# Seven-product block multiplication for the MLP of a one-step decoder layer, with split activations kept in DRAM

## What is computed

```python
x = x + gt1 * mix                                   # mix = merged @ w_out
h = _rmsnorm(x, g2n) * (1 + sc2) + sh2
x = x + gt2 * (jnp.square(jax.nn.relu(h @ w_up)) @ w_down)
...
y_prompt = _rmsnorm(xp, g_final)                    # y_sample the same
```

## Time and profile before

| | us |
|---|---|
| median of 3 runs (1808.34 to 1810.19) | 1808.41 |
| span of the profiled execution | 1804.3 |
| PE busy | 1775.4 (98%) |
| DVE busy | 759.9 (42%) |
| ACT busy | 489.3 (27%) |
| POOL busy | 12.3 (1%) |
| DMA, mean over the span | 77 GB/s |

### The profile page before, as it was taken

The page is one execution under the profiler, slowest core; times in us unless marked ns, Lnnn a source line. Parts: engine busy times, 40 slices in busy tenths (PEclk is TensorE's granted clock), DMA queues, the critical chain, the costliest instruction groups (busy, mean ns, idle before and its releaser), DMA issues.

```text
span 1804.3 us, 26783 instructions
## 1 busy us (share of the span) xinstructions
PE 1775.4 (98%) x10976; PEld 1713.8 (95%) x10976; DVE 759.9 (42%) x1445; ACT 489.3 (27%) x832; POOL 12.3 (1%) x25
## 2 busy tenths in 40 slices
PE   8999999999999999999999989999999999999997
PEld 3899999999999999999999989999999999999997
DVE  3644324444544545333353564343333333433345
ACT  5443333223333233211232341212121121212122
POOL 0000000000000000000000010000000000000000
PEclk9999999999999999999999989999999999999999
DMA  9444544322331232211132111111111111111112
GB/s 310 141 138 156 176 130 131 83 60 69 88 97 54 63 98 58 58 47 46 49 88 79 47 36 47 48 48 46 46 37 45 46 46 46 46 46 46 47 47 97
DMA packets 192677, 139.34 MB, mean 77 GB/s; under 512 B 15323, under 2 KB 176007, under 8 KB 192630
## 3 DMA queue, kind: packets, MB, share of 16 engines
q1 hardware_dynamic: 185910, 130.01, 24.4%
q10 hardware_dynamic: 6720, 8.67, 1.4%
...
## 4 chain that ended last, share of the span: by engine, by line
PE 95%; DVE 2%; DMA 1%; issue 1%; ACT 1%; SPq 0%; DVEq 0%; ACTq 0%
PE PB L916 85%; PE M L844 3%; PE M L969 1%; PE M L860 1%; PE M L1044 1%; DMA araw<-in_w_ada 1%; PE M L1050 1%; PE M L1036 1%; PE M L1038 1%; DVE XL L1223 1%; PE M L908 0%; PE M L1014 0%; DVE R L1709 0%; ACT A L532 0%; PE M L1061 0%
## 5 line engine op out<-in xcount | busy, mean ns | idle before, releaser
L916 PE MATMUL PB<-XH,whi 128*128 128x352 f32 x2496 | 811.3, 325 | 4.1 <-DVE XL L1223 2.1
L916 PE MATMUL PB<-XH,wlo 128*128 128x352 f32 x2496 | 801.5, 321 | 0.0
L916 PE MATMUL PB<-XL,whi 128*128 128x352 f32 x2496 | 801.3, 321 | 0.0
L916 PEld LDWEIGHTS PB<-XH,whi 128*128 128x128 f32 x2496 | 469.0, 188 | 11.3 <-issue 6.9
L916 PEld LDWEIGHTS PB<-XL,whi 128*128 128x128 f32 x2496 | 470.2, 188 | 0.7
L916 PEld LDWEIGHTS PB<-XH,wlo 128*128 128x128 f32 x2496 | 468.7, 188 | 0.0
L550 ACT ACTIVATE whi<-raw 128x1024 fp32r<-128x1024 f32 x134 | 141.3, 1054 | 407.4 <-PE PB L916 404.3
L916 PE MATMUL PB<-AH,whi 128*128 128x352 f32 x720 | 233.1, 324 | 0.2 <-issue 0.2
L916 PE MATMUL PB<-AL,whi 128*128 128x352 f32 x720 | 232.5, 323 | 0.0
L916 PE MATMUL PB<-AH,wlo 128*128 128x352 f32 x720 | 232.1, 322 | 0.0
L1228 DVE TENSOR_TENSOR wlo<-raw,whi 128x1024 fp32r<-128x1024 f32 x134 | 163.7, 1222 | 118.0 <-ACT whi L550 117.1
...
## 6 DMA issues: line engine op xcount, KB each, us to landing
...
```

What stands on the lines that cost most here:

```text
L916: ins = pe.matmul(PB[:, bank, 0:BLK], w[:, w0:w0 + P], x[:, k, a0:a1], start=(k == 0 and j == 0), stop=(k == n_k - 1 and j == 2))
```

## The change

Phase 5 is written anew. The 1056 columns are two halves of 528 (`HALF`), and pairs of feature tiles stand on both sides of a product, so that weights and activations are 2 x 2 blocks. Seven block products replace the eight. With weights A11, A12 (the second half of the inputs), A21, A22 (the second output tile), and inputs B11, B12 (second half of the columns), B21, B22 (second half of the features):

- weight sums (POOL, `sums`, `last_sum`, in place in WR and WS_): S1 = A21 + A22, S3 = A11 - A21, S2 = S1 - A11, S4 = A12 - S2
- input sums: T1 = B12 - B11, T3 = B22 - B12, T2 = B22 - T1, T4 = B21 - T2
- products, numbered 0 to 6: A11 B11, S2 T2, S3 T3, S1 T1, A12 B21, A22 T4, S4 B22. Each is split in high and low and is 2 column parts of 264 (`SUB`) x k-tiles x 3 matmuls (`part`, L1497). There are four accumulators of two banks (`acc`), taken in the order `ACC`: product 4 adds onto 0, 5 onto 2, 6 onto 3.
- results: c11 = acc 0 behind product 4. `s1_copy` (ACT) copies product 0 to UB, `u2` (DVE) adds product 1, `v1` makes U3 = product 2 + UB, `t22` adds product 3 (second tile, second half); `t21` = acc 2 + UB behind product 5, `t12` = acc 3 + UB behind product 6.

**Up** has 16 pairs p (256 inner features each), 4 k-tiles a product: 7 x 24 matmuls. The results B11, B12, B21, B22 get Relu and Square on ACT (`relu2`). POOL makes from them the four differences TB1 to TB4 (`x_sums`, L735), the input sums of the down products. ACT (`bhi`, `thi`) and DVE (`blo`, L2145) split all seven (index XPOS in XS), and SP stores each, 540 KB, to DRAM (`store_x`, L540). **Down** has 8 groups g of 4 pairs d of output tiles (block P0 = 16 + 4g + d), 2 k-tiles a product: 7 x 12 matmuls. Its 14 inputs a group (540 KB each) are loaded back (`load_xd`, L568) into one of two buffers. Results are added in SBUF (AO, UACC). The first column half's residual is read back from DRAM (xm_d, stored in phase 4) by `load_a` (L602) in group 0, the second half's (X2) near the end. Weight parts are 512 (up) or 256 (down) columns, seven a pair.

**Norm.** The sum of squares is now a product of ones with SQA and SQ as the moving side, so that it stands in all partitions, 352 columns; ACT takes the root and DVE the reciprocal over 352 columns (RSTD). DVE and POOL scale A by it and form the seven inputs of the first pairs (`hb`, `xlo`, and the order `XSEQ`); the first pair takes its products in the order `FIRST`. **Output.** All nine row groups stand behind the last product, with four buffers.

The sizes, the transfers, the engines' bodies and TensorE's part (SP, POOL, ACT, DVE, PE in this order):

```diff
+HALF = T // 2
+SUB = HALF // 2
+UP, DOWN = 16, 32
+ACC = (0, 1, 2, 3, 0, 2, 3)
+XPOS = (1, 5, 4, 3, 2, 6, 0)
+FIRST = (0, 4, 2, 1, 3, 5, 6)
+XSEQ = [(0, k) for k in range(4)] + [(4, k) for k in range(4)] + [(i, k) for k in range(4) for i in (2, 1)] + \
...
+        def store_x(p, i, done):
+            sp.wait_ge(s["xl5"], 7 * p + done)
+            sp.dma_start(xd_d[bass.ds(p, 1), :, i + 1, :].rearrange("o p n -> (o p) n"),
+                         XS[:, XPOS[i]].rearrange("p x n -> p (x n)")).then_inc(xbo if done <= 3 else xto, 16)
...
+        def load_xd(g, b, i, free):
+            sp.wait_ge(s["pd5"], free)
+            sp.wait_ge(xbo, 48 * (2 * g + 2 if isinstance(g, int) else UP))
+            sp.wait_ge(xto, 64 * (2 * g + 2 if isinstance(g, int) else UP))
+            for k in range(2):
+                sp.dma_start(xd(b, i)[:, k].rearrange("p x n -> p (x n)").bitcast(F32),
+                             xd_d[bass.ds(2 * g + k, 1), :, i + 1, :].rearrange("o p n -> (o p) n")).then_inc(xdi[b], 16)
...
+        with sp.Fori(1, UP - 1) as p:
+            up(p)
+        p = UP - 1
+        sp.wait_ge(s["wl5"], 7 * UP)
+        load_down(0, 0, 0, 0)
+        load_down(1, 1, 0, 1)
+        store_t(p - 1)
+        for i in range(7):
+            load_xd(0, 0, i, 7 * p + i // 2 + 1)
+            if i == 4:
+                store_x(p, 6, 1)
+        store_x(p, 0, 2)
+        store_x(p, 4, 3)
+        store_t(p)
...
+                sp.dma_start(AO[:, n, 0:HALF], xm_d[n, :, 0:HALF]).then_inc(res_in[d % 2], 16)
...
+                if isinstance(g, int) and g == 0:
+                    load_a(d)
+                    if d == 0:
+                        for i in range(7):
+                            load_xd(1, 1, i, 7 * UP - 7 + (7 + i) // 2 + 1)
+                elif d == 0 and not last:
+                    for i in range(7):
+                        load_xd(g + 1, 1 - b, i, 7 * (P0 - 1) + i + 1)
...
+            pool.tensor_tensor(s1, a(1, 0), a(1, 1), ALU.add).then_inc(s["sum5"], 1)
+            link("sum5", pool.tensor_tensor(a(1, 0), a(0, 0), a(1, 0), ALU.subtract), 4 * P0 + 2)
+            link("sum5", pool.tensor_tensor(s2, s1, a(0, 0), ALU.subtract), 4 * P0 + 3)
...
+            for j, (out, a, b) in enumerate(((TB1, B12, B11), (TB2, B22, B12), (TB3, B22, TB1), (TB4, B21, TB3))):
+                if not first:
+                    pool.wait_ge(s["xl5"], 7 * (p - 1) + 4 + j)
+                if j >= 2:
+                    pool.wait_ge(s["tt5"], 4 * p + 2 * j - 3)
+                pool.tensor_tensor(out, a, b, ALU.subtract).then_inc(s["tt5"], 1)
...
+                x_sums(p - 1)
+            up_sums(p + 1)
+            up_last_sum(p + 1)
...
+            act.activation(RSTD[:, a0:a1], rms_psum(b), ACT.Sqrt, bias=epsc[:, 0:1], scale=1.0 / D).then_inc(s["rms_sqrt"], 1)
...
+        def relu2(p, n, buf):
+            act.activation(buf, buf, ACT.Relu).then_inc(s["rl5"], 1)
+            act.wait_ge(s["rl5"], 3 * p + n)
+            act.activation(buf, buf, ACT.Square).then_inc(s["b5"], 1)
...
+            if not first:
+                up_hi(p, 6)
+                act.wait_ge(s["c12c"], p)
+                relu2(p - 1, 3, B12)
+                s1_copy(p, UB[:])
+                thi(p - 1)
+            w(0)
+            act.wait_ge(s["t22c"], p + 1)
+            if first:
+                act.wait_ge(s["xl2"], len(XSEQ))
+            relu2(p, 1, B22)
+            bhi(p, 6, B22, 1)
+            for i in range(1, 4):
+                w(i)
+            act.wait_ge(s["pd5"], prod(p, 4))
+            if not first:
+                act.wait_ge(s["tt5"], 4 * (p - 1) + 1)
+            act.activation(two(B11), acc(0), ACT.Relu).then_inc(s["c11c"], 1)
+            act.wait_ge(s["c11c"], p + 1)
+            act.activation(B11, B11, ACT.Square).then_inc(s["b5"], 1)
+            bhi(p, 0, B11, 2)
+            w(4)
+            act.wait_ge(s["c21c"], p + 1)
+            relu2(p, 2, B21)
+            bhi(p, 4, B21, 3)
+            w(5)
...
+            dve.reciprocal(RSTD[:, a0:a1], RSTD[:, a0:a1]).then_inc(s["rstd_done"], 1)
...
+            dve.tensor_tensor(two(UB[:]), acc(1), two(UB[:]), ALU.add).then_inc(s["u2c"], 1)
...
+            dve.tensor_tensor(two(B22), acc(2), two(UB[:]), ALU.add).then_inc(s["v1c"], 1)
...
+            dve.tensor_tensor(two(B22), acc(3), two(B22), ALU.add).then_inc(s["t22c"], 1)
...
+            dve.tensor_tensor(two(B21), acc(2), two(UB[:]), ALU.add).then_inc(s["c21c"], 1)
...
+            dve.tensor_tensor(two(B12), acc(3), two(UB[:]), ALU.add).then_inc(s["c12c"], 1)
...
+        def blo(p, i, src):
+            dve.wait_ge(s["xh5"], 7 * p + XPOS[i] + 1)
+            dve.tensor_tensor(XS[:, XPOS[i], 1, :].bitcast(F32R), src, XS[:, XPOS[i], 0, :], ALU.subtract).then_inc(s["xl5"], 1)
...
+            if not first:
+                t12(p - 1)
+                up_lo(p, 6)
+                blo(p - 1, 3, TB1)
+                blo(p - 1, 2, TB2)
+                u2(p)
+                blo(p - 1, 1, TB3)
+                blo(p - 1, 5, TB4)
+                v1(p)
+            w(0)
+            if not first:
+                t22(p)
+            blo(p, 6, B22)
+            for i in range(1, 4):
+                w(i)
+            blo(p, 0, B11)
+            t21(p)
+            w(4)
+            blo(p, 4, B21)
+            w(5)
...
+        def add_gated(n, a):
+            return stt(two(out_half(n, 0)), acc(a), gate(n), two(out_half(n, 0)), ALU.mult, ALU.add)
...
+        FREE = [("c11c", 0), ("u2c", 0), ("c21c", 0), ("c12c", 0), ("s1c", 1), ("v1c", 1), ("t22c", 1)]
...
+        def turn_of(P0, i):
+            pe.wait_ge(s["wl5"], 7 * P0 + i + 1)
+            name, n = FREE[i]
+            if not (isinstance(P0, int) and P0 + n == 0):
...
+        def part(i, u, k, w, x, n_k):
+            for j, (wx, xx) in enumerate(((0, 0), (0, 1), (1, 0))):
+                ins = pe.matmul(acc(ACC[i])[:, u, :], w[wx], x[xx], start=(i < 4 and k == 0 and j == 0),
+                                stop=(k == n_k - 1 and j == 2), skip_group_check=i >= 4)
+            return ins
...
+        def down(g, b):
+            for d in range(4):
+                P0 = UP + 4 * g + d
+                for i in range(7):
+                    if d == 0 and i == 0:
+                        pe.wait_ge(xdi[b], 112 * (g - b) + 224)
+                    turn_of(P0, i)
+                    for u in range(2):
+                        for k in range(2):
+                            ins = part(i, u, k, [d_split(i, x, d % 2)[:, k, :] for x in range(2)],
+                                       [xd(b, i)[:, k, x, SUB * u:SUB * u + SUB] for x in range(2)], 2)
+                    ins.then_inc(s["pd5"], 1)
```

More of the change, by code:

```diff
@@ L504, in layer_kernel @@
+        down(0)
+        down(1)
+        with pool.Fori(1, 3) as t:
+            down(2 * t)
+            down(2 * t + 1)
+        down(6)
+        down(7, last=True)
     POOL_STEPS = 11
@@ L1668, in phase4 @@
                     lo(T4_ + n + 2, x)
[L1669 to L1670 removed]
+                if not (isinstance(i, int) and n == 0):
+                    scaled(n - 1)
                 dve.wait_ge(s["sq_done"], n + 1)
@@ new lines, in _ @@
+        for i in range(6):
+            up_lo(0, i)
+        dve.wait_ge(s["xtr_copy"], KT)
+        residual(KT - 1, 0)
+        scaled(KT - 2)
+        rstd(0)
+        residual(KT - 1, 1)
+        up_lo(0, 6)
+        rstd(1)
+        hb(0, 0)
+        hb(1, 0)
+        residual(KT - 1, 2)
+        xlo(0, 0)
+        hb(2, 0)
+        xlo(0, 1)
+        hb(3, 0)
+        xlo(0, 2)
+        rstd(2)
+        xlo(0, 3)
+        dve.wait_ge(s["rstd_done"], 3)
+        hb(7, 0)
+        hb(0, 1)
```

997 lines of the change are left out of this document (612 added, 385 removed).

## The result

The changed kernel takes 1863.71 us (median of 4 runs, 1858.29 to 1869.97) where the kernel before takes 1808.74; the ratio is 1.0305, 95% interval 1.0282 to 1.0327. The direction was forecast, the size was not: +55 us instead of +8, outside the range that ended at 1836. The profiled execution has a span of 1868.2 us, so it is one of the longer runs.

What follows compares the result with a forecast made beforehand. TensorE's work was taken to bound the kernel before, a three-engine ring the new up loop; -89.5 + 41 + 19 + 18 + 14 + 2.5 + 3 = +8 gave 1816 us, range 1800 to 1828, 8 in 10 1768 to 1836.

Steps and rivals of the forecast that it cites:

- So TensorE sets the pace: Down: a product block takes TensorE 10.1 us, other engines less, and loads at 240 GB/s stay under 360.
- TensorE's work: Whole MLP: 5376 matmuls of 264 columns at 0.1206 us replace 4608 of 352 columns, -89.5 us.
- the hole that was forecast: Down group 0: residual rows stand behind 14 loads for group 1, so TensorE waits, +14 us (+6 to +18).
- the up loop: Up pairs 1 to 15: a three-engine ring takes 22.7 us a pair against TensorE's 20.3, +41 us (+15 to +55).
- the clock: Behind two long gaps the granted clock falls to the 1.2 GHz level for a while, +3 us (0 to +6).
- VectorE's ring: Up loop: path from t12 to next t12 through VectorE, ScalarE and GpSimd, 20.7 us, or 22.7 with locks.
- The stretching by GpSimd: Up loop: VectorE operations with two SBUF inputs wait for whole GpSimd operations, +2.0 us a pair.
- start and bridge: MLP start: norm and first splits, +19 us; between up and down: TensorE waits for 14 loads, +18 us.
- the tail: Behind the last product: all output row groups stand there, 20 us instead of 17.5, +2.5 us (0 to +5).
- Rival 1: Up loop: TensorE still sets the pace, a pair takes 20.7 us, 1769 us in all; chance 0.35.
- Rival 2: Up stores and down loads: DMA becomes the bound below 240 GB/s, bridges grow by 20, 1848 us; chance 0.07.
- Rival 3: TensorE: 264-column matmuls start only every 0.13 us, 27 us more in down, 1843 us; chance 0.04.

Runs made afterwards that it cites:

- Experiment 1: Against the changed kernel, SP issues the 14 loads of the next down group in four portions (4, 4, 4, 2), one behind each block's weight load: 1825.12 us.
- experiment 3: Against the changed kernel, GpSimd's four up weight sums are cut to 2 columns of each 128, values not computed: 1837.74 us, ratio 1.0173.
- experiment 2: Against the changed kernel, VectorE does v1 ahead of the low parts of TB3 and TB4 in the up loop: 1879.20 us, ratio 1.0387.
- experiment 10: Kernel with reordered loads and stores, t22 directly behind v1 and product-by-product waits in group 0, plus GpSimd's up weight sums cut to 2 columns: 1773.43 us.

## Why the prediction was right and wrong

**The step that failed: down, "So TensorE sets the pace".** The prediction compared 9.7 MB in 40.5 us, 240 GB/s, with 360, and put the waits of groups 1 to 7 at nothing. That is an average. The 14 loads of a group were issued in one burst ahead of the weight load of the next block. It then took 15.4 us to land, where 12.6 would have been in time (15.4 less TensorE's 2.75 of idle time). The prediction had the effect in hand: it charged 14 us because group 0's residual rows stand behind 14 loads, and that hole measured 14 with the low clock behind it. It did not ask what else stands behind the same 14 loads in groups 1 to 6. Down cost 55 us over TensorE's work instead of 14 and a part of 3: 29 for the six weight loads, 14 for the hole that was forecast, 6 for a first hole in group 0 (3.25 of idle time and the low clock around it), and 6 for short waits for VectorE in the last group. Experiment 1 shows the first two: 38.6 us from the order alone.

Without the 14 us for the hole the forecast would be 1802, and experiment 1 takes 1825. So a miss of 23 us stays beside the failed step, most of it in TensorE's work (10), the up loop (6) and the rest of down (12, against a part of the clock's 3).

**Mis-sized: the clock,** forecast at 3 us for two long gaps. The low clock costs some 18 us in down alone. Behind each of the six short gaps, of 1.86 to 3.56 us, the granted clock was 0.50, and it added 2.0 us on average to 2.7 of idle time. A gap of such a length does not always bring it: in the up loop nine waits for v1 last 2.39 to 2.53 us, and five of them are followed by the low clock, four are not. TensorE's timeline of two turns (with the low clock the 168 matmuls take 22.26 us):

```profile
1348.24 20.77 PE L1497 MATMUL PS<-XX,WHL 128*128 128x264 f32 x168 [2.48 <-DVE RS L2124]
1371.48 22.26 PE L1497 MATMUL PS<-XX,WHL 128*128 128x264 f32 x168 [2.48 <-DVE RS L2124]
```

In the up loop it costs nothing: both turns are 23.25 us, as VectorE's ring sets them, and the wait behind the slower one is 0.99 instead of 2.48.

**Right: the up loop.** The turn was forecast at 22.7 (20.7 to 23.5) and is 23.25, with TensorE idle some 2.5 us in nine turns (forecast 2.4) and 1 us in those behind a low clock, released by v1, TB4's low part 1.58 (forecast 1.5), the weight part 1.14 (1.1). The stretching by GpSimd, 2.0 us a turn by the prediction's sum, is 1.42 for the weight sums alone (experiment 3), where the sum has 1.2 for them. The share of GpSimd's four differences was not tested by itself. What the prediction had wrong is the reading of v1: it stands in the path as it is written, and experiment 2 shows that taking it out does nothing while t22 is behind the same operations.

**Right: start and bridge.** The splits of the first pair end at 1090.9, and 1086.7 if the 4.2 us ahead of the MLP are taken off; the forecast was 1087. A reciprocal over 352 columns was taken as 3.2 us from a slope between one and four columns, and it is 2.35, three times. The sum holds partly by luck: VectorE takes the last product's first block 3.2 us later than forecast (1029.7 less 4.2, against 1022.3), and still ends the second reciprocal at 1040.7, which is 1036.5 by the same count, where 1036 was forecast. From there to the end of the splits are 50.2 us, forecast 51.

```profile
L2040 DVE RECIPROCAL RS<-RS x3: 2352/2353/2353, 1032.9 to 1049.3; 128x352 f32<-128x352 f32 x3
```

The gap ahead of down was forecast at 18 and is 17.5.

**Mis-sized: TensorE's work.** 264 columns cost 0.1224 us, not 0.1206. It was bounded by 0.1225; over 5376 matmuls it is 10 us. The spacing was worked out from the duration at 258 columns and the drain (0.164) at 352, and an error of 0.002 us a matmul is these 10 us.

**Right: the tail,** +2.3 for +2.5.

**The rivals.** Rival 1 (TensorE still sets the pace of up) does not hold for this kernel: that needs POOL's weight sums away and t22 moved (experiment 10). Rival 2 (DMA becomes the bound, the bridges grow) came nearest with 1848, for the wrong reason: the bridge did not grow, and the bytes were no bound (experiment 1 moves the same). Rival 3 needed 0.13 us a matmul, and 0.1224 was measured. The chances were on the right side by little (0.45 slower, 0.41 faster), and the sign came right with the largest loss put at nothing, so it is in part luck. The range was too short above because no rival held the queue's order.
